# A two-block transformer kernel on one core: table load, first tiles, split order and input order of the first block

## The reference, cut to what is touched

```python
def rmsnorm(x, g):
    y = x32 * lax.rsqrt(jnp.mean(x32 * x32, axis=-1, keepdims=True) + RMS_EPS)
    return (y * g.astype(jnp.float32)).astype(x.dtype)
...
def pool_mixer(h, w_in, w_group, scale):
    u = (h @ w_in).reshape(b, s, POOL_GROUPS, POOL_GROUP_DIM)
    # per group: causal mean over 2, 4, 8 or 16 positions, minus the token
    m = jnp.stack(outs, axis=2)
    y = jnp.einsum('bsgc,gce->bsge', m, w_group).reshape(b, s, d)
    return y * scale
...
hn = rmsnorm(h, norm_mix_g[0]);  h = h + pool_mixer(hn, pool_w_in[0], ...)
hn = rmsnorm(h, norm_ffn_g[0]);  h = h + swiglu(hn, ffn_w_gate[0], ...)
```

## Time and profile before

| | |
|---|---|
| median of 3 runs | 1903.51 us (1899.88 to 1906.83) |
| the profiled execution | 1903.16 us, of which the span is 1901.4 us |
| TensorE busy | 1854.6 us, 98% of the span |
| VectorE, ScalarE, GpSimd busy | 75%, 65%, 5% |
| chain that ended last | TensorE 71%, VectorE 5%, ScalarE 3%, issue 1%, GpSimd 1% |
| moved | 521.10 MB, mean 274 GB/s |
| granted clock of TensorE, mean | 0.994 |

### The profile page before, as it was taken

How to read it: one execution, slowest core, us unless ns; L and a number is a source line. 1 busy time by engine, 2 the same in 40 slices (tenths; PEclk the granted TensorE clock), 3 DMA queues, 4 the chain that set the end, 5 groups by cost and what they waited for, 6 DMA issues and landing times.

```text
span 1901.4 us, 26592 instructions
## 1 busy us (share of the span) xinstructions
PE 1854.6 (98%) x9706; PEld 1539.6 (81%) x9706; DVE 1433.8 (75%) x1241; ACT 1231.3 (65%) x1100; POOL 86.7 (5%) x130
## 2 busy tenths in 40 slices
PE   7999999998999999999999999999999999999998
PEld 6888887886888888888888888888778777888887
DVE  4654567666898988989889898898997766676554
ACT  5543467445877778777787777877767457736452
POOL 0000011011000000000000000000401100000000
PEclk9999999999999999999999999999999999999999
DMA  7974644014999999999999999999985532354551
GB/s 308 358 293 136 219 155 155 25 41 177 414 370 371 406 370 389 368 372 394 370 398 370 373 405 365 391 368 382 378 316 199 189 108 99 111 199 164 194 193 70
DMA packets 76636, 521.10 MB, mean 274 GB/s; under 512 B 8208, under 2 KB 8464, under 8 KB 17296
## 3 DMA queue, kind: packets, MB, share of 16 engines
q1 hardware_dynamic: 72224, 503.27, 68.8%
q0 software_dynamic: 4192, 16.25, 2.2%
q10 hardware_dynamic: 144, 0.52, 0.1%
HBM read 501.14 MB, written 18.87 MB: 273 GB/s over the span
## 4 chain that ended last, share of the span: by engine, by line
PE 71%; DVE 5%; ACT 3%; issue 1%; POOL 1%; DMA 0%; ACTq 0%; DVEq 0%; POOLq 0%
PE bank L919 16%; PE bank L914 16%; PE bank L915 16%; PE bank L553 6%; PE bank L546 6%; PE bank L547 6%; PE bank L936 1%; PE bank L755 1%; DVE w_lo L2032 1%; DVE w_lo L2411 1%; ACT w_hi L1396 1%; POOL small L1902 0%; PE bank L611 0%; PE bank L1187 0%; PE bank L964 0%
## 5 line engine op out<-in xcount | busy, mean ns | idle before, releaser
L2411 DVE TENSOR_TENSOR w_lo<-raw,w_hi 128x2048 fp32r<-128x2048 f32 x336 | 762.0, 2289 | 107.9 <-ACT w_hi L1606 104.2
L1606 ACT ACTIVATE w_hi<-raw 128x2048 fp32r<-128x2048 f32 x336 | 643.1, 1919 | 148.2 <-PE bank L919 148.0
L2032 DVE TENSOR_TENSOR w_lo<-raw,w_hi 128x2048 fp32r<-128x2048 f32 (+2 forms) x136 | 298.2, 2199 | 143.4 <-ACT w_hi L1396 141.7
L1396 ACT ACTIVATE w_hi<-raw 128x2048 fp32r<-128x2048 f32 (+2 forms) x136 | 249.7, 1841 | 162.7 <-PE bank L553 155.1
L914 PE MATMUL bank<-w_hi,xT 128*128 128x512 f32 x896 | 353.6, 395 | 0.0
L915 PE MATMUL bank<-w_hi,xT 128*128 128x512 f32 x896 | 349.2, 390 | 0.0
L546 PE MATMUL bank<-w_hi,xT 128*128 128x512 f32 (+1 forms) x784 | 310.8, 398 | 14.5 <-DVE xT L2753 7.3
L547 PE MATMUL bank<-w_hi,xT 128*128 128x512 f32 (+1 forms) x784 | 304.6, 390 | 0.0
L919 PE MATMUL bank<-w_lo,xT 128*128 128x512 f32 x896 | 240.3, 390 | 1.1 <-DVE w_lo L2411 1.0
L919 PEld LDWEIGHTS bank<-w_lo,xT 128*128 128x128 f32 x896 | 167.9, 188 | 37.7 <-DVE w_lo L2411 2.6
L553 PE MATMUL bank<-w_lo,xT 128*128 128x512 f32 (+1 forms) x784 | 196.1, 392 | 0.0
(11 more groups left out here) (461 smaller groups left out, 1759.4 us busy)
## 6 DMA issues: line engine op xcount, KB each, us to landing
raw<-in_experts_dram SPq DMA_DIRECT2D x336, 1024.0 KB, 6.9
raw<-in_tiles_dram SPq DMA_DIRECT2D x125, 1024.0 KB, 4.8
rows_in<-zeros POOLq DMA_DIRECT2D x1, 6144.0 KB, 32.6
rows_out<-zeros POOLq DMA_DIRECT2D x1, 5632.0 KB, 55.0
raw<-in_tiles_dram SPq DMA_DIRECT2D x9, 512.0 KB, 3.3
item_rows<-rows_in SPq DMA_DIRECT2D x7, 512.0 KB, 7.3
rows_out<-y_s SPq DMA_DIRECT2D x7, 512.0 KB, 3.4
row<-in_rows_dram SPq DMA_DIRECT2D x1, 1040.0 KB, 15.2
```

The source lines that it names most:

```text
L1396: nc.scalar.activation(w_hi[:, i % SPL, 0:kc * w], raw[:, i % DENSE, 0:kc * w], ACT.Copy)\
L1606: nc.scalar.activation(w_hi[:, w_slot(j), :], raw[:, raw_slot(j), :], ACT.Copy).then_inc(m_hi, 1)
L2032: nc.vector.tensor_tensor(w_lo[:, i % SPL, 0:kc * w], raw[:, i % DENSE, 0:kc * w], w_hi[:, i % SPL, 0:kc * w], ALU.subtract).then_inc(spli ...
L2411: nc.vector.tensor_tensor(w_lo[:, s, :], raw[:, raw_slot(j), :], w_hi[:, s, :], ALU.subtract).then_inc(m_lo, 1)
```

## The change

The tile of 512 rows of `pool_in` 0 becomes two of 256, so `pool_in` 0 has five tiles, and every tile behind it has a number higher by one (69 before the experts). ScalarE loads a named function table ahead of its first wait. TensorE runs five products of zeros, 256 columns of float32, ahead of the first tile, once `zeros` is set. `pool_m` and `narrow` get semaphores of their own; TensorE waits for `pool_m` before `mix(0)`, and for `setup` (now `row` and `cst`) before the turn of n1. SP issues tiles 3 to 5 ahead of `h`, tile 6 ahead of `pool_m`, tile 7 ahead of `row` and `cst`, tiles 8 and 9 ahead of `narrow`. ScalarE takes the squares of `h` behind the split of the first tile of `pool_in` 1, not the second, and splits the first `gate` tile ahead of the copies of `mix` 2 and 3. VectorE, at n1, writes `xT2` of the first half ahead of the split of that tile, and runs `pool_add(1)` right behind that split.

```diff
--- before.py
+++ after.py
@@ -132,7 +132,7 @@
                     pieces.append(tiles[j])
 
     for c in range(2):
-        put(block(("pool_in", c), "pool_w_in", c * CB, CB, D, first_sizes=() if c else (1, 1, 2)))
+        put(block(("pool_in", c), "pool_w_in", c * CB, CB, D, first_sizes=() if c else (1, 1, 2, 2, 2)))
     for c in range(2):
         put((("pool_out", c), [("pool_w_group", 2 * c, 0, 4, 256)]))
     for hf, (f0, blocks) in enumerate(FF_HALVES):
@@ -395,6 +395,8 @@
         first_in = sem("first_in")
         narrow_split = sem("narrow_split")
         setup = sem("setup")
+        pool_m_in = sem("pool_m_in")
+        narrow_in = sem("narrow_in")
         x_in = [sem(f"x_in{i}") for i in range(3)]
         h_in = sem("h_in")
         x_split = sem("x_split")
@@ -497,7 +499,7 @@
         batches, batch_of = [], {}
         groups, group_of = [], {}
         tiles_done = []
-        SETUP = 4 * 16
+        SETUP = 2 * 16
 
 
         @block.tensor
@@ -1242,10 +1244,13 @@
                             last = nc.tensor.matmul(o, x1, b1, start=False, stop=k == 1)
                 last.then_inc(used, 1)
 
+            pe.wait_ge(zeros_set, 1)
+            for _ in range(5):
+                nc.tensor.matmul(acc[0][:, 0:S], zeros[:, 0:P], zeros[:, 0:S], start=True, stop=True)
             gemm(("pool_in", 0), "A", xT1, xT2, ready=lambda ch: pe.wait_ge(x_split, ch + 1))
             begin(("pool_in", 1), "A")
             tile(("pool_in", 1), 0, xT1, xT2)
-            pe.wait_ge(setup, SETUP)
+            pe.wait_ge(pool_m_in, 16)
             pe.wait_ge(acc_free["A"], 1)
             mix(0)
             mix(1)
@@ -1254,6 +1259,7 @@
             pe.wait_ge(acc_free["A"], 2)
             mix(2)
             mix(3)
+            pe.wait_ge(setup, SETUP)
             turn_norm("n1", h, (0,), (h_done, 2))
             pool_out(1)
             gate0, up0 = ("gate", 0, 0), ("up", 0, 0)
@@ -1310,14 +1316,16 @@
             sp.dma_start(x_T[:, 2:4, :].rearrange("p a b -> p (a b)"), t["x_T"][:, 2 * S:4 * S]).then_inc(x_in[1], 16)
             load(range(2, 3))
             sp.dma_start(x_T[:, 4:8, :].rearrange("p a b -> p (a b)"), t["x_T"][:, 4 * S:8 * S]).then_inc(x_in[2], 16)
-            load(range(3, 4))
+            load(range(3, 6))
             sp.dma_start(h[:], t["x"][0].rearrange("(t p) d -> p t d", p=P)).then_inc(h_in, 16)
-            load(range(4, 6))
-            sp.dma_start(pool_m[:].rearrange("p a b c -> p (a b c)"), t["pool_mix"]).then_inc(setup, 16)
+            load(range(6, 7))
+            sp.dma_start(pool_m[:].rearrange("p a b c -> p (a b c)"), t["pool_mix"]).then_inc(pool_m_in, 16)
+            load(range(7, 8))
             sp.dma_start(row[:], t["rows"].broadcast_to((P, N_ROW))).then_inc(setup, 16)
             sp.dma_start(cst[:], t["consts"]).then_inc(setup, 16)
-            sp.dma_start(narrow[:].rearrange("p a b -> p (a b)"), t["narrow"]).then_inc(setup, 16)
-            load(range(6, cbs["dn_out", 1][1]))
+            load(range(8, 10))
+            sp.dma_start(narrow[:].rearrange("p a b -> p (a b)"), t["narrow"]).then_inc(narrow_in, 16)
+            load(range(10, cbs["dn_out", 1][1]))
             sp.wait_ge(o_normed, 3)
             sp.dma_start(mem_in[:, :, :], t["mem_2"][0].rearrange("(t p) d -> p t d", p=P)).then_inc(mem_loaded, 16)
             load(range(cbs["dn_out", 1][1], NA))
@@ -1370,6 +1378,7 @@
 
         @block.scalar
         def _(act):
+            nc.scalar.preload_act_table_set("natural_log_exp_and_others")
             act.wait_ge(first_in, 16)
             told = {}
             state = {"split": 0, "limit": NA, "own": 0, "hi": 0}
@@ -1831,23 +1840,26 @@
 
             for k in range(KD):
                 x_high(k)
-                split_to({0: 1, 1: 2, 3: 3, 7: 4}.get(k, 0))
-            split_to(cbs["pool_in", 1][1])
+                split_to({0: 1, 1: 2, 3: 3, 5: 4, 7: 5}.get(k, 0))
+            split_to(cbs["pool_in", 1][0] + 1)
             act.wait_ge(h_in, 16)
             norm_squares("n0", h)
+            split_to(cbs["pool_in", 1][1])
             norm_used("n0")
             for c in range(2):
                 banks = after(("pool_in", c))
                 for tt in range(NT):
                     tell(nc.scalar.activation(pool_u[:, tt, c * CB:c * CB + CB], banks[tt][:, :], ACT.Copy,
                                               scale=root("n0", tt)), acc_free["A"] if tt else a_own)
+                if c:
+                    split_to(cbs["pool_out", 1][1] + 1)
                 for g in (2 * c, 2 * c + 1):
                     b = batch(("pool", g))
                     tell(nc.scalar.activation(mix1[:, 2 * g:2 * g + 2, :], b[:, :].rearrange("p (a b) -> p a b", a=2),
                                               ACT.Copy), hi_out)
             transition("n1", "ffn0", group_of["pool_out", 1][1], lambda: act.wait_ge(h_done, 4))
             norm_used("n1")
-            act.wait_ge(setup, SETUP)
+            act.wait_ge(narrow_in, 16)
             tell(nc.scalar.activation(narrow_hi[:, :, :], narrow[:, :, :], ACT.Copy), narrow_split)
             last_up = None
             for hf, (f0, blocks) in enumerate(FF_HALVES):
@@ -2782,7 +2794,13 @@
             pool_add(0)
             mix_low(2)
             mix_low(3)
-            transition("n1", "ffn0", cbs["pool_out", 1][1], lambda: pool_add(1))
+            norm_turn("n1", "ffn0", halves=(0,))
+            split_to(cbs["pool_out", 1][1] + 1)
+            pool_add(1)
+            split_to(cbs["pool_out", 1][1] + 3)
+            norm_turn("n1", "ffn0", halves=(1,))
+            split_to(cbs["pool_out", 1][1] + 4)
+            norm_used("n1")
             dve.wait_ge(narrow_split, 1)
             nc.vector.tensor_tensor(narrow_lo[:, :, :], narrow[:, :, :], narrow_hi[:, :, :], ALU.subtract)\
                 .then_inc(narrow_split, 1)
```

## The result

| | kernel before | changed kernel |
|---|---|---|
| median | 1903.72 us (1899.88 to 1908.37, 6 runs) | 1893.83 us (1891.07 to 1894.85, 6 runs) |
| ratio | | 0.995, 95% interval 0.9935 to 0.9964 |
| profiled execution, span | 1903.16, 1901.4 us | 1893.50, 1891.5 us |
| TensorE busy | 1854.6 us | 1854.7 us |

The changed kernel is faster, by 9.9 us in this comparison. So the change is worth 6 to 10 us. Where in this range a comparison falls is a matter of the clock: of 29 executions of the kernel before on one chip, those with a mean granted clock of 0.992 took 1905.7 us on average and those with 0.996 took 1898.8. TensorE's busy time is the same and its idle time 10.0 us less, but 4.5 us of the busy time are now products of zeros.

What follows compares the result with a forecast made beforehand. TensorE, busy 98% of the span, was taken to bound the kernel. 4.3 us at norm n0 plus 2.15 at `gate` is 6.4; 1903.2 less 6.4 gives 1896.8 us, range 1892.5 to 1902.0.

Steps and rivals of the forecast that it cites:

- Part 1, the start: At the start, early table load and hidden products of zeros let TensorE start tile 2 at 9.8, finish tile 5 at 23.4.
- Part 2, the data: Input transfers take 2.5 us per MB, halved tiles cost nothing extra and just suffice, `h` lands at 17.2.
- Rival (a): At the start, `h` or a tile lands 2.5 us late and all of it is lost: 1899.3 us; chance 0.18.
- Part 3, the norm: At norm n0, squares start when `h` lands, so `mix(0)` starts at 23.5 instead of 27.76: 4.3 us.
- Part 4, `gate`: At norm n1, earlier `xT2` starts `gate` at about 46.55, not 48.70 (old clock): 2.15 us; two short waits stay.
- The sum's end of 7.5: Upper end of the gain, if the two short waits (on `pool_add(0)` and `mix_low(3)`) before `gate` go as well.
- Part 5, the expert loads: At the first expert loads, shifted slots make load four wait like the seventh; charged nothing, bound 0 to 12.6 us.
- The prediction's sign: Among the signs of being right: splits of expert tiles are still released by TensorE; no size given.
- Rival (b): At the start, products of zeros don't raise the clock: 1.7 us less gain, 1898.5 us; chance 0.10.
- Rival (c): At the start, the table load stays before the first `x_high`: 0.1 to 0.9 us less gain, 1897.3; chance 0.07.
- The sum: Gain by `gate`: 4.3 at norm n0 plus 2.15 at norm n1 is 6.4 us, ends 3.9 and 7.5.
- a few us either way: In later stretches, a shifted start can move losses of granted clock after idle time by this much.

Runs made afterwards that it cites:

- the repeats: The changed kernel run twice more with no edit: 1895.57 us (6.1 less than the kernel before) and 1894.82 us (7.3 less).
- the trace with the filler: The changed kernel plus two float32 products of 512 columns, in no result, at the wait before the memory's keys: 1894.75 us, ratio 0.9963.
- the warm start: The kernel before with only the early table load and the five products of zeros: 1904.23 us, ratio 1.001.
- the changed kernel with the old order: The changed kernel with ScalarE's and VectorE's order at norm n1 put back as before: 1897.33 us, ratio 0.9968.
- its yardstick: The changed kernel with no edit, run a third time, beside the last group of kernels on the same chip: 1894.82 us, ratio 0.996.

## Why the prediction was right

The time (1893.83 against 1896.8, inside the range) and the sign were right. The mechanism carries the 6.4 us at `gate`; that the first comparison gave 9.9 us and not 6.4 is luck of the clock, and the repeats (6.1 and 7.3) are nearer. By its own steps:

- **Part 1, the start.** Right in mechanism. The zeros end at 6.4 as worked out (1.88 plus 4.51), the spacing is 0.23 from the second real product on. The third tile's split starts at 8.82, not 8.6, since its own data landed then, after a wait of 0.24. The first chunk of `x_T` landed 0.8 us later in this run than in the trace of before; in the other traces it landed between 4.59 and 5.16.
- **Part 2, the data.** 2.5 us per MB held. Landings were 0.4 us behind the list (15.10 for 14.7, 17.66 for 17.2). The one real miss is tile 8, whose split started on landing at 30.81 where 29 was forecast, and at 30.67 and 30.45 in the repeats; why it is late is open. It is used by `pool_out(1)`, which didn't wait for it. Rival (a) fell: `h` was 0.4 late, not 2.5.
- **Part 3, the norm.** 4.63 us from the squares to `pool_u` (forecast 4.65), `mix(0)` at 23.84, 23.42 and 23.93 in three traces (forecast 23.5), 3.9 us gained for 4.3. The norm chain is last there, but only just, as the prediction had it. Where the products are last, `mix(0)` follows the start of their last eight by 1.81 or 1.82 us; here it is 1.95, so they have 0.14 us to spare with the zeros (none in the trace with the filler) and are late without them.
- **Part 4, `gate`.** 2.19 us more, no wait, both short waits still there. Tile 9's split ends at 35.58, 0.8 us ahead of the copy at 36.41. The sum's end of 7.5 counts the two short waits as 1.1 us; they were 0.41 and 0.45 before, which makes 7.3.
- **Part 5, the expert loads.** Right, at nothing. Here three loads, not six, go out at first, and the fourth waits 12.6 us. Its split starts 6.71 us earlier than in the earlier trace rows, which is the gain of this stage, and waits for nothing: it follows ScalarE's own work (the table load of 478.56 ends there). The prediction's sign, splits of expert tiles released by TensorE, holds for the later ones (145.9 of the 146.1 us that these splits waited in all). Queue of SP and ScalarE, changed kernel:

```profile
456.10 1.28 SPq L1310 DMA_DIRECT2D raw<-in_experts_dram  x3
```
```profile
SPq L1310 <- DVE w_lo L2044: 12.6, 1, 12.6
```
```profile
479.85 1.92 ACT L1615 ACTIVATE w_hi<-raw 128x2048 fp32r<-128x2048 f32 x1
```

- **Rival (b), that zeros don't raise the clock,** fell: they do. What failed is its price of 1.7 us. The step behind it took 5.3 us, from the one trace of before, as the time the lower level lasts; it was 3.1 and 5.0 us in the two runs without zeros, which made 0.4 and 1.2 us.
- **Rival (c)** gave 0.1 to 0.9 us for the preload; 0.5 measured.
- **The sum.** 6.4 forecast at `gate`; 6.1, 6.6, 6.0 and 6.6 in the four traces that have the whole change (6.1 in the profiled execution of the result). The 3.7 us between these 6.1 and the 9.8 at the end of the trace are the term that the prediction left at "a few us either way". Of them 2.0 came behind the wait shown above and 1.1 between 1540 and 1600, where the level fell at other places and waits took part of it up. The other 0.6 came by the first expert load; 0.4 of it is no clock but a wait that was shorter (2.53 us before 437.82 in the kernel before, 2.16 at the same place after), for a reason that stays open.

Undone one at a time, the parts cost 6.3 to 6.8 (squares), 2.2 (turn), 1.8 (large tile, `mix(0)` 3.33 us behind `pool_u` instead of 1.55), 0.5 (preload) and 0.4 to 1.2 (zeros), together more than the whole 6.1 to 6.6: norm, supply of tiles and clock level meet at `mix(0)`, and the one that is late takes the others' gain with it. Put in alone, the halved tile and the warm start were each worth nothing or less. The prediction had both paths meet at 23.5 and said that neither alone could give more. The runs of single parts agree for the supply and the level; the norm's part alone was not run.

## What to carry to other kernels

When an engine waits for the later of two chains, work out both ends and shorten them together: here a faster supply alone brought nothing and lost 0.1%, and with the squares of the norm back behind a split (two lines of code) 2.0 us of the gain were left, not clear of the noise. Judge an edit of 0.1% by the distance between two events of one trace (`pool_u` to `mix(0)`), in more than one trace, not by medians, which differ by up to 1.7 us for the same kernel (1893.83, 1894.82, 1895.57). And look past the edit in the trace: a gain that grows in a stretch which the edit doesn't touch is the clock's, and may not be there the next time.

## What was not expected of the hardware

- **The lower level at the start has no fixed length:** 3.1 us (5.98 to 9.11) and 5.0 us (5.95 to 10.94) after the first product in two runs of one kernel; 3.1 in two other kernels with the start of before (7.25 to 10.35 with the halved tile) and over 5 in the trace of before. And it isn't in the granted clock of the record. The stretch of the second, in which products lie 0.43 us apart (columns: stretch, length, busy us and count of TensorE, its weight loads, VectorE, ScalarE, GpSimd, then granted clock, share of DMA, GB/s):

```profile
6.00:9.00 3.00, 3.00 (x7) 2.42 (x8) 2.41 (x6) 2.67 (x5) 0.00 (x0) 1.00 1.02 411
```

- **Equal waits, unequal levels.** A wait of a given length doesn't settle whether the level falls behind it:
  - at `gate`, it held behind 2.07 us in the trace of before and behind 2.08 in the changed kernel with the old order, and fell behind 2.08 in the kernel before with the halved tile alone and with the warm start alone;
  - at the last expert item (1.7 us) it fell in three of 14 traces;
  - near 1486 (1.5 us) it fell in the trace with the filler and held in its yardstick's;
  - for `pool_u`, it held behind 2.38 and 2.39 us, and behind 2.59 and 4.35 it had fallen at the first product;
  - at the memory's keys (2.7 us) it had fallen at the first product in the first trace of the changed kernel, and fell about 1 us later in the repeats. Behind 0.8 us, with the filler, it held.

  One such fall costs about 1.5 to 2 us (2.0 in the last expert item, 1.5 near 1486). What sets the moment was not found.
